# One queue for all pages: cached keys and values of a decoder step fetched by the SP queue alone

## The reference

```python
mod = jnp.dot(jax.nn.silu(c), w_ada) + b_ada
h = rmsnorm(x, g_pre1) * (1.0 + sc1) + sh1
proj = jnp.dot(h, w_in)                       # 1024 x 5632
hq, hf, hi, hg, aq, ak, av, ua, ub = jnp.split(proj, splits, axis=-1)
o_a, s_new = hgrn2_recurrence(...)            # gated linear recurrence, 4 heads
k_past = cache_k[l][page_table]               # pages chosen by a table
v_past = cache_v[l][page_table]
# q . k over all positions; blocks of 256 scored by q . mean(k), the best 3 and the own one kept
o_b = moba_attend(q, k_all, v_all, pos)       # one softmax, then p . v; 8 heads of 64
merged = sigmoid(ua) * jnp.dot(o_a, w_proj_a) + sigmoid(ub) * jnp.dot(o_b, w_proj_b)
x = x + gt1 * rmsnorm(jnp.dot(merged, w_out), g_post1)
# then the SwiGLU block: w_gu (1024 x 5632), w_down (2816 x 1024)
```

## Time and profile before

| | |
|---|---|
| median of three runs | 857.01 us (856.23 to 857.40) |
| the profiled execution | 857.27 us, span 855.6 us |
| TensorE busy | 760.3 us, 89% of the span |
| DVE, ACT, POOL busy | 470.0, 318.9, 98.7 us |
| read from HBM | 163.44 MB, 197 GB/s over the span |

### The profile page before, as it was taken

The page is one execution under the profiler, slowest core; times in us unless marked ns, Lnnn a source line. Parts: engine busy times, 40 slices in busy tenths (PEclk is TensorE's granted clock), DMA queues, the critical chain, the costliest instruction groups (busy, mean ns, idle before and its releaser), DMA issues.

```text
span 855.6 us, 14654 instructions
## 1 busy us (share of the span) xinstructions
PE 760.3 (89%) x5263; PEld 652.4 (76%) x5263; DVE 470.0 (55%) x551; ACT 318.9 (37%) x432; POOL 98.7 (12%) x132
## 2 busy tenths in 40 slices
PE   5749999999998899999599787899389999999995
PEld 2328878887898799999554233799289999999994
DVE  2785445544574966767633772474844544544425
ACT  3545554456545211110212131343344554543422
POOL 2341000000100404540011111000020000000000
PEclk9589999999999999999856697899679999999998
DMA  9764666566644787787775989956115555444401
GB/s 326 250 203 150 232 235 219 196 211 211 204 139 138 218 250 214 228 244 237 226 275 190 334 271 326 348 186 197 50 50 161 172 157 164 163 164 145 150 1 56
DMA packets 103471, 168.80 MB, mean 197 GB/s; under 512 B 6449, under 2 KB 37865, under 8 KB 103298
## 3 DMA queue, kind: packets, MB, share of 16 engines
q1 hardware_dynamic: 85778, 137.68, 49.0%
q10 hardware_dynamic: 14368, 19.87, 7.9%
q0 software_dynamic: 3280, 10.64, 3.3%
HBM read 163.44 MB, written 4.72 MB: 197 GB/s over the span
## 4 chain that ended last, share of the span: by engine, by line
PE 79%; DVE 10%; DMA 4%; ACT 3%; issue 2%; SPq 1%; POOL 0%; ACTq 0%; DVEq 0%
PE ps L1267 16%; PE ps L1269 16%; PE ps L1268 16%; PE ps L1403 13%; PE ps L1417 3%; DVE w_lo L835 2%; DMA ring<-cache_v 2%; PE ps L1279 2%; PE ps L1448 2%; DMA xtok<-x_sample 2%; PE ps L1608 1%; PE ps L1479 1%; PE ps L1290 1%; PE ps L1280 1%; ACT w_hi L505 1%
## 5 line engine op out<-in xcount | busy, mean ns | idle before, releaser
L835 DVE TENSOR_TENSOR w_lo<-ring,w_hi 128x1024 fp32r<-128x1024 f32 x174 | 209.1, 1238 | 125.9 <-ACT w_hi L505 123.8
L1267 PE MATMUL ps<-h_hi,w_hi 128*128 128x288 f32 x704 | 212.6, 302 | 19.4 <-POOL h_lo L387 18.6
L505 ACT ACTIVATE w_hi<-ring 128x1024 fp32r<-128x1024 f32 (+1 forms) x176 | 177.7, 1043 | 118.2 <-PE ps L1269 108.3
L1268 PE MATMUL ps<-h_lo,w_hi 128*128 128x288 f32 x704 | 209.6, 298 | 0.0
L1269 PE MATMUL ps<-h_hi,w_lo 128*128 128x288 f32 x704 | 209.0, 297 | 0.0
L1267 PEld LDWEIGHTS ps<-h_hi,w_hi 128*128 128x128 f32 x704 | 133.9, 190 | 24.4 <-POOL h_lo L387 19.1
L1269 PEld LDWEIGHTS ps<-h_hi,w_lo 128*128 128x128 f32 x704 | 134.4, 191 | 0.0
L1268 PEld LDWEIGHTS ps<-h_lo,w_hi 128*128 128x128 f32 x704 | 134.1, 190 | 0.1
L1403 PE MATMUL ps<-KT,Wq 128*128 128x128 f32 x1024 | 121.0, 280 | 7.4 <-DVE KT L958 7.4
L1403 PEld LDWEIGHTS ps<-KT,Wq 128*128 128x128 f32 x1024 | 118.7, 196 | 8.7 <-issue 4.1
L958 DVE STREAM_TRANSPOSE KT<-ring 128x2048 f32<-128x2048 f32 x32 | 73.8, 2308 | 36.5 <-PE ps L1403 36.1
(11 more groups left out here) (281 smaller groups left out, 941.0 us busy)
## 6 DMA issues: line engine op xcount, KB each, us to landing
ring<-w_ada SPq DMA_DIRECT2D x24, 1024.0 KB, 5.3
ring<-cache_k SPq DMA_DIRECT2D x96, 256.0 KB, 3.5
ring<-w_in SPq DMA_DIRECT2D x22, 1024.0 KB, 5.6
ring<-w_gu SPq DMA_DIRECT2D x44, 512.0 KB, 4.7
ring<-cache_v SPq DMA_DIRECT2D x64, 256.0 KB, 4.8
ring<-w_down SPq DMA_DIRECT2D x10, 1024.0 KB, 5.0
ring<-cache_k ACTq DMA_DIRECT2D x32, 256.0 KB, 3.5
ring<-cache_v POOLq DMA_DIRECT2D x32, 256.0 KB, 5.2
```

Of the source, the lines that this page charges most:

```text
L505: act.activation(w_hi[:, par, k, :], slot4(s)[:, k, :], ACT.Copy).then_inc(sem("hi_split"), 1)
L835: dve.tensor_tensor(w_lo[:, par, k, :], slot4(s)[:, k, :], w_hi[:, par, k, :].bitcast(F32), ALU.subtract).then_inc(sem("lo_split"), 1)
L1267: pe.matmul(dst, h, x_hi, start=first, stop=False)
L1268: pe.matmul(dst, h, x_lo, start=False, stop=False)
```

## The change

SP fetches all four pages of each slot, of keys and of values. ACT and POOL fetch none, and their waits for free slots go with the fetches. TensorE waits for one semaphore per value slot where it waited for two.

```diff
@@ SP
-                load_pages(sp, "cache_k", 0, j, range(3), "k_landed")
+                load_pages(sp, "cache_k", 0, j, range(4), "k_landed")
             with sp.Fori(1, NSEQ) as b:
                 for j in range(4):
                     sp.wait_ge(sem("key_slots"), b * 4 + (j - 3))
-                    load_pages(sp, "cache_k", b, j, range(3), "k_landed")
+                    load_pages(sp, "cache_k", b, j, range(4), "k_landed")
 
             for j in range(4):
                 sp.wait_ge(sem("key_slots"), 4 * NSEQ - 3 + j)
-                load_values(sp, j, j, range(2), "v_landed", 0)
+                load_values(sp, j, j, range(4), "v_landed", 0)
@@ SP, the loop over the other 28 slots of values
-                        load_values(sp, r * 4 + j, j, range(2), "v_landed", group)
+                        load_values(sp, r * 4 + j, j, range(4), "v_landed", group)
@@ POOL
-            for j in range(4):
-                pool.wait_ge(sem("key_slots"), 4 * NSEQ - 3 + j)
-                load_values(pool, j, j, [3], "v3_landed", 0)
-            for group in range(2):
-                with pool.Fori(4 * group + (group == 0), 4 * group + 4) as r:
-                    for j in range(4):
-                        pool.wait_ge(sem("value_slots"), r * 4 + (j - 3))
-                        load_values(pool, r * 4 + j, j, [3], "v3_landed", group)
@@ ACT: keys(), value_pages() and their calls between its other steps are gone
-                if h == 0:
-                    value_pages(3, 3)
-                else:
-                    value_pages(4 + (h - 1) // 2, 2 * ((h - 1) % 2), 2 * ((h - 1) % 2) + 1)
@@ TensorE, values()
-                pe.wait_ge(sem(f"v_landed{j}"), 48 * (b + 1))
-                pe.wait_ge(sem(f"v3_landed{j}"), 16 * (b + 1))
+                pe.wait_ge(sem(f"v_landed{j}"), 64 * (b + 1))
```

More of the change, by code:

```diff
@@ L568, in _ @@
             hi_a(43)
[L570 to L574, removed]
-                    else:
-                        act.wait_ge(sem("key_slots"), 4 * b + j - 3)
-                    load_pages(act, "cache_k", b, j, [3], "k_landed")
             hi_a(44)
             act.wait_ge(sem("table_landed"), 16)
-            keys(0, 0)
             evac_in(9, 43)
@@ L587, in _ @@
             act.activation(vtok[0:TSA, 2, :], ps[0:TSA, 6, :], ACT.Copy).then_inc(sem("v_tok"), 1)
-            keys(0, 1)
             act.activation(proj[:, HF:HF + 4, :], proj[:, HF:HF + 4, :], ACT.Sigmoid).then_inc(sem("sig_f"), 1)
-            keys(0, 2)
             evac_in(10, 45)
-            keys(0, 3)
             act.wait_ge(sem("k_turned_tok"), 1)
@@ L605, in _ @@
             act.activation(hkt[:, :, :], proj[:, HF:HF + 4, :], ACT.Ln).then_inc(sem("logf"), 1)
-            keys(1, 0, 1)
             act.wait_ge(sem("b_ready"), 1)
             act.activation(hqt[:, :, :], hb[:, :, :], ACT.Exp).then_inc(sem("eb"), 1)
-            keys(1, 2)
             act.wait_ge(sem("kd_ready"), 1)
@@ L621, in level_exp @@
                 act.activation(hx[li % 2][:, :, 0:r], hx[li % 2][:, :, 0:r], ACT.Exp).then_inc(sem("lv_exp"), 1)
-            keys(1, 3)
             level_exp(0)
-            keys(2, 0)
             scores(0)
             level_exp(1)
-            keys(2, 1, 2, 3)
             act.wait_ge(sem("h_turned"), 1)
@@ L634, in _ @@
             act.activation(hvs[:, :, :], ps[0:TSA, 7, :].rearrange("p (h d) -> p h d", h=HH), ACT.Copy).then_inc(sem("h_tok"), 1)
-            keys(3, 0)
             scores(1)
@@ L639, in _ @@
                 if b > 2:
-                    keys(b + 1, 0)
                     scores(b - 1)
@@ L643, in _ @@
                         level_exp(2 * b - 3)
-                keys(b + 1, 1, 2)
                 if 2 * b - 2 < 7:
                     level_exp(2 * b - 2)
-                keys(b + 1, 3)
             scores(6)
[L650 to L659, removed]
             act.wait_ge(sem("d_done"), 1)
             act.activation(D0[:, :, :], ps[:, 2, :].rearrange("p (h d) -> p h d", h=HH), ACT.Copy).then_inc(sem("d0_ready"), 1)
-            value_pages(0, 1, 2, 3)
             scores(7)
@@ L669, in _ @@
                 act.activation(S[:, b, :], S[:, b, :], ACT.Exp, bias=stat[:, 304 + b:305 + b], accum_out=stat[:, 320 + b:321 + b]).then_inc(sem("s_exp"), 1)
-            value_pages(1, 0, 1, 2, 3)
-            value_pages(2, 0, 1, 2)
             act.wait_ge(sem("o_done"), 1)
@@ L677, in _ @@
             act.activation(hx[0][:, :, :], hb[:, :, :], ACT.Square).then_inc(sem("o_sq"), 1)
-            value_pages(2, 3)
-            value_pages(3, 0)
             act.wait_ge(sem("o_sum"), 1)
@@ L683, in _ @@
             act.activation(hx[1][:, :, SAMP], ps[:, 6, 0:HH * TSA].rearrange("p (h d) -> p h d", h=HH), ACT.Sqrt, scale=1.0 / DK, bias=C("eps")).then_inc(sem("o_root"), 1)
-            value_pages(3, 1, 2)
             act.wait_ge(sem("state_p"), 1)
```

## The result

| | before | after |
|---|---|---|
| median | 856.62 us (4 runs, 853.73 to 857.40) | 898.19 us (4 runs, 896.09 to 900.13) |
| ratio, 95% interval | | 1.0491 (1.0454 to 1.0528) |
| profiled execution, span | 857.27, 855.6 us | 899.43, 897.6 us |

The forecast was 896.8 us, with a range of 885 to 910 us.

A forecast was written before the change was run, and what follows sets the result against it. SP's issue rate was taken to bound the values, with TensorE bounding the keys before. Terms: 0 (ACT and POOL) + 3 (keys) + 36.5 (values) = 39.5 us on 857.27 us, so 896.8 us; range 885 to 910 us.

The forecast's parts named there:

- SP's page and turn: Both SP page loops: 1.165 us per bare page, 19.79 us per turn, 4.95 us per slot.
- Keys, 3 us: Key stage: SP slower than TensorE's slots despite its lead, so the end of the keys moves about 3 us.
- The first values and the states, hidden: Between the loops: 16 value pages hidden by 14.3 us of softmax work, the states' DMAs hidden by under 1 us.
- Values, 36.5 us: Value loop: SP runs through without slot waits, last page at 571.0 us; 36.5 us of w_proj_a's 39.5 us delay.
- The tail behind them: Last value slot to line 1267: 1.5 us plus 4.5 us, ending at 580.6 us; every later wait as before.
- The rival of the transfers: Cached-page stages: transfers are the limit and issue costs nothing beside them; 857 us, chance 0.03.
- The rival "faster": Value slots: one paced queue brings slow landings back to the median, 8.2 us less, 849 us; chance 0.02.
- cheap loop: SP's loops: 18.64 us per turn, w_proj_a 29.8 us later, 887 us (880 to 888 us); chance 0.12.
- dearer: SP's loops at 20.6 us per turn, TensorE's clock lower in the keys; 913 us (905 to 920 us), chance 0.11.
- What would show it: Profile signs: DMA starts 1.16 to 1.3 us apart, cache_v waits above 35 us, values near 212 GB/s, unchanged 314.5 us end.

The follow-up runs named there:

- double read: The changed kernel with each page number read twice, the first read unused; 1029.91 us (one run).
- the experiment with keys alone: The kernel before with only the keys' fourth page moved to SP, values still on three queues; 858.61 us against 854.33 us, ratio 1.0049.
- one queue with cheap requests: The changed kernel with SP reading a slot's four page numbers in one load, without the bounds check; 858.56 us against 854.33 us, ratio 1.0041.

## Why the prediction was right, step by step

- **SP's page and turn** (1.165 us, 19.79 us per turn): right. The profile after has the first pages of two turns of the key loop at 292.13 and 311.73 us, 19.6 us apart, and 137.5 us for each loop against 136.5 us by the forecast. The double read shows that this time counts in full.
- **Keys, 3 us:** 4.0 us by the profile, 4 us by the experiment with keys alone. The last transposition began at 412.24 us against the forecast 411.5 us: the loop began 0.9 us later than before and took 0.5 us more, and its last page landed 0.7 us sooner.
- **The first values and the states, hidden:** right for the values, which started 14.3 us behind the end of the keys, as before. The states were not hidden: TensorE waited 1.08 us for them, since their DMAs were issued from 427.98 to 433.49 us and not up to 432 us as forecast, and landed in 7.2 us (median; 6.4 us before). It cost nothing at the end. The first four slots took 4.97 us instead of 6.57 us, so line 1427 began at 439.44 us, 3.6 us later than before and no later than the stage as a whole, and SP sets the end of the values.
- **Values, 36.5 us:** right in mechanism, a little small. The last page was issued at 572.74 us against 571.0 us, w_proj_a at 573.30 us against 572.1 us. In the loop SP waited for no slot.
- **The tail behind them:** the step that was mis-sized. I let the last slot, its sums and the turn take what they took before, 4.5 us behind the value matmuls; they took 6.2 us, and the last slot 1.93 us where I had allowed 1.5 us, because TensorE was at its lower clock level. The forecast for the first projection matmul was 580.6 us, the result 584.60 us. Of these 4.0 us, 1.7 us lie in the sums and the turn and 0.4 us in the last slot; the others are the last page, issued 1.7 us later than forecast and landed 0.2 us more slowly. The rest of the kernel took 313.0 us instead of the same 314.5 us, which hid 1.5 us and was luck: it goes with the moment at which the clock rises again. Before, the projection's matmuls stayed at the lower level (0.44 us each instead of 0.30 us) for 6.1 us, after the change for 4.5 us. In the thirteen traces of this case the rest takes 314.4 to 314.5 us where that time is 6.1 us, and 311.6 to 311.9 us where it is 2.8 to 3.0 us.
- **The rival of the transfers**, with the rule that the Trainium skill states (DMA: Bandwidth & Descriptors, Issuing engines are not separate DMA queues): halving the bytes left the time as it was, so it falls for this kernel. The first half of that rule, that all issuing engines use the same DMA engines, agrees with the traces: three queues kept them busy 0.95 of the time at 331 GB/s (before, 466 to 490 us), one queue with cheap requests 0.95 at 320 GB/s (490 to 541 us), and its time came within 0.4%. "Usually small" is what does not hold here: 1.165 us of issue stood against 0.85 us of transfer for 256 KB.
- **The rival "faster"** was priced at a break-even of 3.61 us per slot. Its mechanism did occur (landings fell from 4.8 to 3.0 us) and was outweighed. The break-even was too high: with 3.71 us per slot SP already cost 12 us, and with 3.29 us about 4 us were left.
- **The rivals "cheap loop" and "dearer":** a turn took 19.6 to 19.7 us, neither 18.64 nor 20.6 us. TensorE's clock did not fall in the keys: its mean granted clock was 1.00 from 303 to 418 us in both kernels, although TensorE now waited for the transpositions there. The lower level cost time behind the values, where no rival had it.
- **What would show it:** four figures were off. TensorE's matmuls waited 29.2 us for `cache_v`, not over 35 us; line 1365 was busy 54.6 us instead of 44.2 us, at a lower mean clock, and so took 10.4 us of what would have been idle time. Landings fell below the 3.5 us named. The keys ended at 418.44 us, just behind the 417 to 418 us named. The stretch behind the values, which was to stay the same, changed by 1.5 us; the forecast had named a change there as a sign of being wrong. What it had wrong there is the clock, which its sum held at the old level.

## What to carry to other kernels

A queue that issues is an engine with a rate: count the DMAs per stage, take the step between two starts where it does not wait (here 1.165 us with a table read, 0.51 us without), and compare it with the fastest stretch in which the buffers come free, not with the mean: with a mean of 3.61 us per slot, 3.71 us on SP already cost 12 us, since the last eight slots came every 3.13 us. Before spreading fetches over engines, or gathering them on one, make each request cheap: one load for all page numbers of a slot, without the check of bounds, gave back 37 of the 41 us that the two missing queues had cost.

## What the runs showed of the hardware

- A load of one number from the table into a register took SP 0.27 us, a load of four 0.87 us; the saving lies as much in the register steps and the check of bounds that went with each single load (0.55 us in all for one read).
- A DMA instruction takes SP 0.33 to 0.34 us (median) whether it moves 256 KB or 128 KB. Single ones took up to 1.07 us in the changed kernel and 1.58 us where starts were 0.51 us apart.
- TensorE was granted its lower clock level for much of a stage that waited for data (0.58 on average from 466 to 577 us). Waiting is not the whole of it: in the kernel before, from 428.6 to 466 us, TensorE was busy 37.33 of 37.4 us and the mean granted clock was 0.55. The first matmuls of the projection were at the lower level in both kernels, for 6.1 us before and 4.5 us after, and the profile charges this to a later stage.
